# Attention maps of two heads side by side in TensorE, with mask and maximum in one VectorE instruction

## The reference

```python
# forgetting attention (4 heads of 64, stage mix1)
logits = einsum('bhqd,bhkd->bhqk', q, k) * scale + c_blk[..., :, None] - cum[..., None, :]
p = softmax(where(causal, logits, -inf)); out = p @ v
# differential attention (4 heads, two maps of 32 each, stage mix1)
p = attn_map(q1, k1) - lam * attn_map(q2, k2); out = p @ v
# memory attention, no mask (mem1: 4 heads of 256; xa0, xa1: 4 heads of 128)
# banded attention with sinks and a bias by distance (8 heads of 64, stage mix2)
m = maximum(max(logits, -1), s); e = exp(logits - m); p = e / (sum(e, -1) + exp(s - m))
# latent attention over the chosen keys (8 heads of 128, stage mix2): bias and a second mask
# 16 heads, two gated branches of 64 and a compressed one (stage mix3)
```

## Time and profile before

| | us |
|---|---|
| median of 3 runs | 2657.49 (2647.33 to 2663.75) |
| profiled execution | 2651.68 |
| its span, first instruction to last | 2649.9 |
| TensorE busy | 2356.4 (89%) |
| DVE busy | 1630.2 (62%) |
| ACT busy | 1265.9 (48%) |

### The profile page before, as it was taken

How to read it: one execution, slowest core, us unless ns; L and a number is a source line. 1 busy time by engine, 2 the same in 40 slices (tenths; PEclk the granted TensorE clock), 3 DMA queues, 4 the chain that set the end, 5 groups by cost and what they waited for, 6 DMA issues and landing times.

```text
span 2649.9 us, 31609 instructions
## 1 busy us (share of the span) xinstructions
PE 2356.4 (89%) x12540; PEld 1846.6 (70%) x12540; DVE 1630.2 (62%) x1835; ACT 1265.9 (48%) x1372; POOL 106.2 (4%) x89
## 2 busy tenths in 40 slices
PE   8977697999889887997889869999999999999995
PEld 7965686333568577996755757777778777878774
DVE  4436453111435656775057668878888888888885
ACT  4343342111233534443225347767676767666662
POOL 3002000000000001221000000000000000000000
PEclk9979897999888898998959879999999999999997
DMA  8430125999643024554600249989999999989892
GB/s 272 153 96 1 64 80 192 417 413 416 228 126 125 17 80 160 182 181 151 147 0 1 80 170 361 343 316 343 336 347 328 340 336 328 357 309 361 314 359 108
DMA packets 285683, 592.17 MB, mean 223 GB/s; under 512 B 12123, under 2 KB 118015, under 8 KB 277248
## 3 DMA queue, kind: packets, MB, share of 16 engines
q1 hardware_dynamic: 280000, 571.54, 60.9%
q0 software_dynamic: 5568, 19.06, 2.3%
...
## 4 chain that ended last, share of the span: by engine, by line
PE 74%; DMA 10%; ACT 6%; DVE 6%; issue 3%; POOL 0%; SPq 0%; DVEq 0%; ACTq 0%
PE psF L997 9%; PE psF L999 9%; PE psF L998 9%; PE psB L997 8%; PE psB L998 8%; PE psB L999 8%; DMA ring<-in_moe_w_gate_dram 4%; DMA ring<-in_w_dram 4%; PE psF L1169 3%; PE psB L1204 3%; PE psF L1331 2%; PE psB L1353 2%; ACT arena_rounded L1753 2%; PE psB L1052 1%; PE psF L1182 1%
## 5 line engine op out<-in xcount | busy, mean ns | idle before, releaser
L2252 DVE TENSOR_TENSOR ring_rounded<-ring,arena_rounded 128x2048 fp32r<-128x2048 f32 x224 | 507.0, 2287 | 29.5 <-ACT arena_rounded L1753 29.2
L1753 ACT ACTIVATE arena_rounded<-ring 128x2048 fp32r<-128x2048 f32 x224 | 429.5, 1919 | 196.2 <-DMA ring<-in_moe_w_up_dram 135.3
L997 PE MATMUL psF<-arena_rounded 128*128 128x512 f32 x896 | 360.4, 402 | 3.4 <-ACT arena_rounded L1775 1.5
L999 PE MATMUL psF<-arena_rounded 128*128 128x512 f32 x896 | 355.6, 397 | 0.0
L998 PE MATMUL psF<-ring_rounded,arena_rounded 128*128 128x512 f32 x896 | 354.6, 396 | 0.0
L1965 DVE TENSOR_TENSOR ring_rounded<-ring,ring_rounded 128x2048 fp32r<-128x2048 f32 (+1 forms) x71 | 153.9, 2171 | 191.4 <-ACT ring_rounded L1607 191.3
L997 PEld LDWEIGHTS psF<-arena_rounded 128*128 128x128 f32 x896 | 170.2, 190 | 44.2 <-issue 4.9
L999 PEld LDWEIGHTS psF<-arena_rounded 128*128 128x128 f32 x896 | 169.6, 189 | 39.7
L998 PEld LDWEIGHTS psF<-ring_rounded,arena_rounded 128*128 128x128 f32 x896 | 169.8, 190 | 37.7
L1607 ACT ACTIVATE ring_rounded<-ring 128x2048 fp32r<-128x2048 f32 (+1 forms) x71 | 128.5, 1812 | 118.0 <-PE psF L999 80.7
L998 PE MATMUL psB<-ring_rounded,PT_rounded 128*128 128x512 f32 x448 | 178.2, 398 | 0.0
...
## 6 DMA issues: line engine op xcount, KB each, us to landing
...
```

What stands on the lines that cost most here:

```text
L997: mm(bank, x1, w1, start=start, stop=False)
L999: return mm(bank, x2, w1, start=False, stop=stop)
L1753: ap_(w_hi[slot].bitcast(R32), ring[:, slot], ACT.Copy).then_inc(q["high"], 1)
L2252: V.tensor_tensor(ring_r[:, slot].bitcast(R32), ring[:, slot], w_hi[slot], ALU.subtract)\
```

## The change

Maps with 64 value columns are taken two at a time, as a bundle; maps with wider values stay single. Four things follow.

TensorE's logits of a bundle alternate between the two maps, which lie on different rows of the array (64 rows each, or 32 for the differential maps) and go to different banks, now F[0] to F[3]. Its value products alternate too, on columns 0 to 63 and 64 to 127 of one output bank. Transposes stay one after another and go to B[2] and B[3]. To make partners of different halves, the differential maps and those of mix3 change their order.

On DVE, masks of other than forgetting maps are added and the row maximum found by one `tensor_tensor_reduce` for each 256 columns; it leaves the negated sum of logits and mask in the buffer, and the exponential takes its scale of -1 for it. Latent maps add the first mask separately, as before. Maps without a mask are not copied: DVE takes the maximum from PSUM, and the exponential reads PSUM. Reciprocal, coefficient and sink come once for a bundle.

There are six map buffers and four for transposed maps in mix1, mix2 and mix3, the additional ones in parts of the arena that are unused there. Waits change with them: logits wait for the maximum (or the exponential) of four maps earlier, in place of `scored` two maps earlier.

Lags are in bundles now: transposes two behind the logits, values three behind, and `inputs_attended` five behind its group.

```diff
-        NS = 3
-        S, S_r = sb_rounded("S", [P, NS, TT, T])
+        NS = 6
+        S, S_r = sb_rounded("S", [P, 3, TT, T])
...
+        more_at = {"mix1": r.at}
...
+        more_s = {stage: Region(at).get(3, TT, T) for stage, at in more_at.items()}
+        more_pt = {stage: Region(0 if stage == "mix2" else at + 3 * TT * T).get(2, TT, T) for stage, at in more_at.items()}
...
+            bundles[stage], m = [], m0
+            while m < len(maps):
+                two = maps[m]["v"].shape[2] == 64
+                bundles[stage].append((m, m + 1) if two else (m,))
+                m += 2 if two else 1
+            for m in range(m0, len(maps)):
+                maps[m].update(stage=stage, at=m - m0)
+
+        def s_of(m):
+
+            mp = maps[m]
+            if mp["stage"] not in more_s:
+                return S[:, mp["at"] % 3], mp["at"] % 3
+            n = mp["at"] % NS
+            return (S[:, n] if n < 3 else more_s[mp["stage"]][:, n - 3]), n
+
+        def s_count(m):
+            return NS if maps[m]["stage"] in more_s else 3
+
+        def pt_of(m):
+            mp = maps[m]
+            n = mp["at"] % 4
+            if mp["stage"] not in more_s:
+                return PT[:, n % 2]
+            return PT[:, n] if n < 2 else more_pt[mp["stage"]][:, n - 2]
+
+        def pt_count(m):
+            return 4 if maps[m]["stage"] in more_s else 2
...
-                        coef=neglam if c else None, v=dv[:, :, 64 * j:64 * j + 64], base=64 * (j % 2))
-        diff = [([diff_map(j, c) for j in (2 * a, 2 * a + 1) for c in range(2)], yT[:, 2 + a, :]) for a in range(2)]
+                        coef=neglam.unsqueeze(1).broadcast_to([P, 2, TT]) if c else None, v=dv[:, :, 64 * j:64 * j + 64], base=64 * (j % 2))
+        diff = [([diff_map(j, c) for c in range(2) for j in (2 * a, 2 * a + 1)], yT[:, 2 + a, :]) for a in range(2)]
...
-        attention("mix3", [(nsa_maps(2 * a) + nsa_maps(2 * a + 1), yT[:, a, :]) for a in range(8)])
+        attention("mix3", [([nsa_maps(j)[branch] for branch in range(2) for j in (2 * a, 2 * a + 1)], yT[:, a, :])
+                           for a in range(8)])
...
-            def logits(m):
...
+            def logits(bundle):
+
+                for m in bundle:
+                    if maps[m]["at"] >= 4:
+                        pe.wait_ge(max_ready if "mask" in maps[m] else exp_ready, m - 3)
                 for t in range(TT):
-                    n = len(mp["qk"]) + (TT if "fox" in mp else 0)
...
+                    n = len(maps[bundle[0]]["qk"]) + (TT if "fox" in maps[bundle[0]] else 0)
+                    for i in range(n):
+                        for m in bundle:
+                            mp, bank = maps[m], F[maps[m]["at"] % 4]
+                            if i < len(mp["qk"]):
+                                q, k = mp["qk"][i]
+                                q = q[:, P * t:P * t + P]
+                            else:
+                                st = i - len(mp["qk"])
+                                q = nlogf[:, st, mp["fox"]:mp["fox"] + 1].broadcast_to([P, P])
+                                k = tri[:, st, :]
+                            last = mm(bank[:, T * t:T * t + T], q, k, start=(i == 0), stop=(i == n - 1))
+                            if t == TT - 1 and i == n - 1:
+                                last.then_inc(logits_ready, 1)
 
             def transpose_probs(m):
                 pe.wait_ge(probs_ready, m + 1)
-                if m >= 2:
+                if maps[m]["at"] >= 2:
                     pe.wait_ge(pt_saved, m - 1)
                 for k in range(TT):
                     for t in range(TT):
-                        last = nc.tensor.transpose(F[2 + m % 2][:, T * k + P * t:T * k + P * t + P],
-                                                   S[:, m % NS, t, P * k:P * k + P], eye)
+                        last = nc.tensor.transpose(B[2 + m % 2][:, T * k + P * t:T * k + P * t + P],
+                                                   s_of(m)[0][:, t, P * k:P * k + P], eye)
                 last.then_inc(pt_ready, 1)
 
-            def values(m):
...
+            def values(bundle):
+
+                for m in bundle:
+                    mp = maps[m]
+                    g = mp["group"]
+                    if mp["new"] and g >= 2:
+                        pe.wait_ge(o_saved, g - 1)
+                    if mp.get("compressed") is not None:
+                        j = mp["compressed"]
+                        rows = slice(32 * (j // 2 % 4), 32 * (j // 2 % 4) + N_CMP)
+                        mm(B[g % 2][mp["base"]:mp["base"] + 64, 0:T], vc4[rows, j // 8, :], pcT[rows, j % 2, j // 8, :],
+                           start=True, stop=False)
+                pe.wait_ge(pt_saved, bundle[-1] + 1)
+                width = maps[bundle[0]]["v"].shape[2]
                 for piece in range(0, width, P):
                     w = min(P, width - piece)
                     for k in range(TT):
-                        last = mm(bank[base:base + w, 2 * piece:2 * piece + T], mp["v"][:, k, piece:piece + w],
-                                  PT[:, m % 2, k, :], start=(first and k == 0), stop=(mp["last"] and k == TT - 1))
-                last.then_inc(pv_done, 1)
+                        for m in bundle:
+                            mp = maps[m]
+                            first = mp["first"] and mp.get("compressed") is None
+                            last = mm(B[mp["group"] % 2][mp["base"]:mp["base"] + w, 2 * piece:2 * piece + T],
+                                      mp["v"][:, k, piece:piece + w], pt_of(m)[:, k, :],
+                                      start=(first and k == 0), stop=(mp["last"] and k == TT - 1))
+                            if piece + P >= width and k == TT - 1:
+                                last.then_inc(pv_done, 1)
 
             def attend(stage):
-                m0, m1, _, _ = map_span[stage]
...
+                todo = bundles[stage]
+                for i in range(len(todo) + 3):
+                    if i < len(todo):
+                        logits(todo[i])
+                    if 0 <= i - 2 < len(todo):
+                        for m in todo[i - 2]:
+                            transpose_probs(m)
+                    if 0 <= i - 3:
+                        values(todo[i - 3])
                 pe.wait_ge(o_saved, groups_end(stage))
...
             def exps(m):
-                mp, s = maps[m], m % NS
+                mp, (buf, n) = maps[m], s_of(m)
                 act.wait_ge(max_ready, m + 1)
+                if "mask" not in mp:
+                    src, sign = pair(F[mp["at"] % 4]), 1.0
+                    if mp["at"] >= s_count(m):
+                        act.wait_ge(pt_ready, m - s_count(m) + 1)
+                else:
+                    src, sign = buf, 1.0 if "fox" in mp else -1.0
                 if "sink" in mp:
                     j = mp["sink"]
-                    ap_(esink[:, s], nmx[:, s], ACT.Exp, bias=sinks[:, j:j + 1])
+                    ap_(esink[:, n], nmx[:, n], ACT.Exp, bias=sinks[:, j:j + 1])
                 for t in range(TT):
-                    ins = ap_(S[:, s, t], S[:, s, t], ACT.Exp, bias=nmx[:, s, t:t + 1], accum_out=ssum[:, s, t:t + 1])
+                    ins = ap_(buf[:, t], src[:, t], ACT.Exp, bias=nmx[:, n, t:t + 1], scale=sign,
+                              accum_out=ssum[:, n, t:t + 1])
                 ins.then_inc(exp_ready, 1)
 
             def save_probs(m):
                 act.wait_ge(pt_ready, m + 1)
-                if m >= 2:
-                    act.wait_ge(pv_done, m - 1)
-                ap_(PT[:, m % 2], pair(F[2 + m % 2]), ACT.Copy).then_inc(pt_saved, 1)
+                if maps[m]["at"] >= pt_count(m):
+                    act.wait_ge(pv_done, m - pt_count(m) + 1)
+                ap_(pt_of(m), pair(B[2 + m % 2]), ACT.Copy).then_inc(pt_saved, 1)
...
-            def score_map(m):
...
+            def score_bundle(bundle):
+
+                for m in bundle:
+                    mp, (buf, n) = maps[m], s_of(m)
+                    bank = pair(F[mp["at"] % 4])
+                    dve.wait_ge(logits_ready, m + 1)
+                    if "mask" not in mp:
+                        V.tensor_reduce(nmx[:, n], bank, AX.X, ALU.max, negate=True).then_inc(max_ready, 1)
+                        continue
+                    if mp["at"] >= s_count(m):
+                        dve.wait_ge(pt_ready, m - s_count(m) + 1)
+                    if "fox" in mp:
+                        j = mp["fox"]
+                        for t in range(TT):
+                            ins = V.scalar_tensor_tensor(out=buf[:, t], in0=bank[:, t], scalar=cumq[:, t, j:j + 1],
+                                                         in1=mp["mask"][:, t], op0=ALU.add, op1=ALU.add)
+                        do(ins)
+                        ins = V.tensor_reduce(nmx[:, n], buf, AX.X, ALU.max, negate=True)
+                    else:
+                        more = mp["mask"]
```

(40 more changed lines are left out.)

101 lines of the change are left out of this document (18 added, 83 removed).

## The result

| | before | after |
|---|---|---|
| median | 2652.41 us (4 runs, 2635.46 to 2663.75) | 2570.19 us (4 runs, 2563.55 to 2571.14) |
| profiled execution | 2651.68 | 2570.84 |
| its span | 2649.9 | 2569.0 |

The ratio is 0.969, with a 95% interval from 0.9632 to 0.9748.

What follows compares the result with a forecast made beforehand. TensorE was taken to bound the six attention stages. Gains of 38 us (mix3), 9.5 (mix2), 8 (mix1) and 4.5 (mem1, xa0, xa1) sum to 60: 2651.7 becomes 2592, plus 5.8 for the median, 2598; range 2574 to 2623.

Steps and rivals of the forecast that it cites:

- TensorE's pairs: In a bundle, both overlaps whole: two maps' logits cost 1.05 us and values 1.01, as one map's did before.
- Rival (b): Paired matmuls on TensorE go one after the other, step 5.2 us, gain 10 to 20: 2642 us; chance 0.06.
- DVE's instruction: Mask and maximum in one instruction: 0.42 + 0.04 us each, 0.92 a map for 1.33, a bundle 3.3 us.
- Rival (a): DVE sets the step in mix3, mix1 and mix2, its instruction at 0.75 us each: 2615 us; chance 0.08.
- The step of mix3: One bundle in mix3 takes 3.5 us at 2.4 GHz, with all three engines at 3.2 to 3.45.
- Fill and drain: At the ends of mix3, where the pipeline fills and empties: 7 us of idle time.
- At equal clock: mix3 without its clock term: sixteen steps of 3.5 us, 56, plus 7 idle.
- mem1, xa0 and xa1: Stages without pairs: 1.7 us gained in each xa and 1 in mem1, 4.5 together (1 to 6).
- the window maps: Eight maps of mix2, 27 us before, as four bundles take 20 with fill and slow clock: 7 gained.
- the latent maps: Eight single maps of mix2, at 2.8 us each for 3.15 before: 2.5 us gained.
- The clock: mix3's slow stretch at 1.2 GHz lasts 26 us (bounds 7 and 40), which adds 13 us to the stage.
- Rival (c): TensorE waits more and the clock stays at 1.2 GHz through all six stages: 50 us slower, 2707; chance 0.06.

Runs made afterwards that it cites:

- the run with halves apart: The changed kernel with TensorE working through a bundle one map after the other, bundles, buffers and DVE's instruction kept: 2653.93 us, ratio 1.0015 to the kernel before.

## Why the prediction was right in kind and 22 us short

- **TensorE's pairs** (1.05 for the pair's logits, 1.01 for its values): right, 1.06 and 1.02. Rival (b), matmuls that go one after the other, is out, and with it the gain would be nil, as the run without overlap shows, not 10 to 20 us.
- **DVE's instruction**: 0.42 us each was forecast, 0.42 is measured. The 0.04 added for the read was wrong, since reads lie under the next instruction: 0.345 apiece, 2.9 us a bundle for 3.3. PSUM as a source costs nothing: 419 ns from PSUM, 422 from SBUF. Rival (a) is out; DVE sets the step only if it keeps two instructions.
- **The step of mix3**: 3.5 forecast, 3.66 measured. TensorE's part was right; ACT's copy, called covered, is late in every second bundle. The Trainium skill's rule, in TensorEngine Tiling (Array Packing), Performance Considerations, that emptying PSUM may become the bottleneck (it says so of a fourfold speed-up of TensorE) is borne out in this small measure, by ACT and not by DVE.
- **Fill and drain**: 7 us beside the sixteen steps were forecast for mix3; 61.5 us at equal clock less 16 x 3.66 leave 3. TensorE's idle time is 6.6 us (60 less 53.40), but about half of it lies in the steps.
- **At equal clock** mix3 was to take 56 + 7 = 63 us and takes 61.5 (63.4 less half of 3.8). That it fits so well is luck in part: the steps were 2.6 us too short and the ends 4 too long. mix1 gained 8.8 at equal clock (51.5 - 9.7 less 35.4 - 2.4) for 8; mix2 9.4 for 9.5 (in which the clock was counted); mem1, xa0 and xa1 1.7 + 2.0 + 2.0 = 5.7 for 4.5. In mix2 the two parts were off in opposite ways: the window maps end 15.6 us after the start (849.75 to 865.35) where 20 was forecast, and the latent maps gained 1.5 for 2.5.
- **The clock: the step that failed.** "I take 26, the mean of 19, 17 and 40", with "the bounds ... 7 us and the 40 us of now", for the slow stretch of mix3. It was 3.8 us, which made that term 1.9 us instead of 13; and mix1's, which the sum left as it was, shrank from 19.4 to 4.8 us. The sum held 7 us for the clock (and a few in mix2, not kept apart); it was 29 by the trace. These 22 us are all that was missing in the two profiled executions (81 gained for 60): the other terms came to 52 (55.8 less the 3.9 outside the stages), where the forecast had 53. The forecast of 2598 was another 5 us too high, because the kernel before had its median at 2652.4 and not at 2657.5. What stood behind it was the idea that the length of a slow stretch belongs to the stage, as a given. The runs show that it belongs to what TensorE does in it: with logits in pairs the clock came back 3 to 4 us into mix3 and stayed in seven of the eight traces of kernels built that way, while the one with DVE's two instructions, whose TensorE waits more, needed 20. With single logits in the bundles' order it came back after 3 us too, but fell at the end of the fill and needed another 20. mix1's 4.8 us is less firm: its first slow stretch was 5 us in all eight, but in five of them the clock fell again, and those had 15 to 22 us in all.
- **Rival (c)**, the clock, had the right item with the wrong sign. It reasoned from idle time alone: a TensorE that waits more keeps a lower clock. Waiting does play a part in the falls, as the fill of the run with halves apart shows. But the rows that spoke against it as the whole cause were there: TensorE was busy for 38.72 of 40 us at 0.50, so it was not waiting that held the clock down in single maps.
- **Buffers** had no price of their own in the prediction. They are worth 17 us. The waits above show where; my reading, which no run tests by itself, is that steps that alternate between 3.1 and 4.2 us, with three engines busy for 79 to 89% of the time, need room.
- **Slips in its sums**: the mean of 19, 17 and 40 is 25, not 26; two maps of mix3 at 1.2 GHz are 2 x 4.95 + 1.04 = 10.9 us, not 10.5; and 5 us below 2581 is 2576, not 2574. None changes the outcome.

**What stays open.** Why work on all rows goes with an early return of the clock, while pairs of columns don't, is not settled; the runs show the relation, not its cause. Nor is it settled when the clock falls again. It fell a second time in mix1 in five of the eight traces with logits in pairs, in mix2 in all, and stretches of one kernel differ by 10 us and more between executions. Nor is it known why mix1 was slow for 63 and 57 us with single logits in the bundles' order, and for only 19 in the kernel before.
